# Routing moved into the output stage of a decoder block, tile by tile, with its slot table summed on TensorE

## What is computed

```
xn = rms_norm(h);  proj = xn @ w_in                       # 1024 -> 4352
m  = sigmoid(g_a) * (swa(q_a,k_a,v_a) @ P_a) + sigmoid(g_b) * (stick_breaking(q_b,k_b,v_b) @ P_b)
h  = h + m @ w_out
h  = h + moe_ffn(rms_norm(h))

moe_ffn: logits = x @ router_w + router_b                 # 32 experts
         top_logit, top_idx = top_k(logits, 4);  gate = softmax(top_logit)
         per expert e and its tokens:
             gu = x @ w_gate_up[e] + b_gate_up[e]         # 1024 -> 2048
             act = (clip(u, -7, 7) + 1) * (min(g, 7) * sigmoid(1.702 * min(g, 7)))
             out[token] += gate * (act @ w_down[e] + b_down[e])
```

## Time and profile before

| | |
|---|---|
| median of 3 runs | 2639.85 us |
| the profiled execution | 2638.29 us, its span 2636.7 us |
| mean granted TensorE clock | 0.946 |
| TensorE busy | 2372.2 us (90%) |
| VectorE busy | 1606.5 us (61%) |
| ScalarE busy | 1310.4 us (50%) |
| GpSimd busy | 907.4 us (34%) |
| HBM read and written | 480.34 MB, 47.56 MB |

### The profile page before, as it was taken

The page is one execution under the profiler, slowest core; times in us unless marked ns, Lnnn a source line. Parts: engine busy times, 40 slices in busy tenths (PEclk is TensorE's granted clock), DMA queues, the critical chain, the costliest instruction groups (busy, mean ns, idle before and its releaser), DMA issues.

```text
span 2636.7 us, 39181 instructions
## 1 busy us (share of the span) xinstructions
PE 2372.2 (90%) x13878; PEld 1822.8 (69%) x13879; DVE 1606.5 (61%) x1526; ACT 1310.4 (50%) x1453; POOL 907.4 (34%) x654
## 2 busy tenths in 40 slices
PE   6989999999998889029999999999999999999995
PEld 5857768777786768017777777777777777777774
DVE  4034353544423432727878887878888878777785
ACT  4145454554534421025655665556566556555554
POOL 1210101011011100762545454545465535434453
PEclk9988989999898989559999999999999999999998
DMA  3000201111114432348888998889899888887884
GB/s 128 25 25 21 65 22 41 47 30 58 36 57 156 138 136 104 94 150 307 323 290 304 344 326 290 303 297 367 280 367 347 280 290 319 291 281 273 298 303 149
DMA packets 277825, 524.72 MB, mean 199 GB/s; under 512 B 39041, under 2 KB 87228, under 8 KB 277596
## 3 DMA queue, kind: packets, MB, share of 16 engines
q1 hardware_dynamic: 244028, 476.21, 50.9%
q0 software_dynamic: 22208, 43.38, 6.9%
q10 hardware_dynamic: 11520, 4.20, 0.6%
HBM read 480.34 MB, written 47.56 MB: 200 GB/s over the span
## 4 chain that ended last, share of the span: by engine, by line
PE 41%; POOL 6%; issue 5%; DMA 3%; ACT 1%; DVE 1%; POOLq 0%; DVEq 0%; ACTq 0%
PE ex_gu L1790 23%; PE ex_yp L1834 8%; PE ex_rest L1812 4%; DMA ex_nxt<-slots 3%; PE ex_rest L1851 2%; POOL ex_idx L1576 2%; PE ex_gu L1783 1%; POOL slots L1563 1%; ACT ex_whi L1491 1%; POOL ex_nxt L1571 1%; POOL ex_sel L1618 1%; PE ex_tr L1751 1%; DVE ex_hlo L1681 1%; PE ex_yp L1827 0%; ACT ex_hhi L1510 0%
## 5 line engine op out<-in xcount | busy, mean ns | idle before, releaser
L1648 DVE TENSOR_TENSOR ex_wlo<-ex_raw,ex_whi 128x2048 fp32r<-128x2048 f32 x355 | 804.6, 2291 | 179.1 <-ACT ex_whi L1491 177.9
L1491 ACT ACTIVATE ex_whi<-ex_raw 128x2048 fp32r<-128x2048 f32 x387 | 736.0, 1920 | 311.9 <-PE ex_gu L1790 224.4
L1790 PE MATMUL ex_gu<-ex_whi,ex_xhi 128*128 128x512 f32 x1024 | 333.9, 407 | 5.4 <-DVE ex_wlo L1648 5.4
L1790 PE MATMUL ex_gu<-ex_wlo,ex_xhi 128*128 128x512 f32 x1024 | 321.0, 395 | 0.0
L1790 PE MATMUL ex_gu<-ex_whi,ex_xlo 128*128 128x512 f32 x1024 | 319.6, 393 | 0.0
L603 POOL TENSOR_TENSOR at_wlo<-at_raw,at_whi 128x1024 fp32r<-128x1024 f32 x32 | 79.6, 2487 | 583.8 <-ACT at_whi L448 583.8
L1629 POOL TENSOR_TENSOR ex_wlo<-ex_raw,ex_whi 128x2048 fp32r<-128x2048 f32 x32 | 148.0, 4625 | 251.9 <-ACT ex_whi L1491 251.9
L1790 PEld LDWEIGHTS ex_gu<-ex_whi,ex_xhi 128*128 128x128 f32 x1024 | 192.2, 189 | 58.0 <-DVE ex_wlo L1648 7.4
L1790 PEld LDWEIGHTS ex_gu<-ex_whi,ex_xlo 128*128 128x128 f32 x1024 | 193.9, 189 | 43.9
L1790 PEld LDWEIGHTS ex_gu<-ex_wlo,ex_xhi 128*128 128x128 f32 x1024 | 193.6, 189 | 42.9
L56 PE MATMUL at_job<-xnT_hi,at_whi 128*128 128x512 f32 x448 | 196.1, 438 | 0.0
(11 more groups left out here) (256 smaller groups left out, 4198.7 us busy)
## 6 DMA issues: line engine op xcount, KB each, us to landing
ex_raw<-in_w_gate_up_dram SPq DMA_DIRECT2D x512, 512.0 KB, 7.0
ex_raw<-in_w_down_dram SPq DMA_DIRECT2D x256, 512.0 KB
at_raw<-in_w_in_dram SPq DMA_DIRECT2D x28, 512.0 KB
gT<-at_gst SPq DMA_DIRECT2D x32, 256.0 KB, 2.4
mg_g<-gT SPq DMA_DIRECT2D x32, 256.0 KB, 3.1
n_x<-in_x_dram SPq DMA_DIRECT2D x8, 512.0 KB, 8.1
mg_ytok<-y_s SPq DMA_DIRECT2D x16, 256.0 KB, 4.2
raw_o<-in_w_out_dram SPq DMA_DIRECT2D x8, 512.0 KB, 6.6
```

The lines of the kernel that those rows point to most:

```text
L1491: nc.scalar.activation(w_hi[:, i % RING, :], raw[:, i % SLABS, :], ACT.Copy).then_inc(hi_d, 1)
L1648: nc.vector.tensor_tensor(w_lo[:, slot, :], raw[:, i % SLABS, :], w_hi[:, slot, :].bitcast(F32), ALU.subtract).then_inc(lo_d, 1)
L1790: mm = nc.tensor.matmul(gu[:, half, h, :], x[:, k, :], w[:, kk, h, :], start=k == 0 and n == 0, stop=k == KD - 1 and n == 2)
```

## The change

Routing is no longer a stage. Its parts go to four places. In `project_values` GpSimd makes the bias pieces, which are stored to HBM and loaded again in the expert stage. In the output stage each tile is routed as soon as its logits are there: `choose` (top 4, one-hot rows), `rank_tokens` (ranks on TensorE), `hand_out` (weights, and the one-hot matrix of slots) and `take_slots`, four float32 products that add (token, weight) at (expert, slot) into a table in PSUM. The slots of an expert up to its 160th are then on the chip, and `next_rows` copies them instead of loading them. The table of further blocks (`further_table`, `destinations`) is computed by VectorE in expert blocks 0 and 1, and the 32 scatters to HBM are issued four at a time in blocks 2 to 9; they are read only in block 30. The merge has seven buffers for eight, `us` and `us2` are gone (their contents stand in `hid`, `hid2`).

```diff
 (project_values, sync and gpsimd)
             def _(sp):
                 load_first_tiles(sp, w_in, raw, raw_in)
+                for q in range(3):
+                    sp.dma_start(brow[q * NE:(q + 1) * NE, 0:2 * D], b_gate_up[0, :, :]).then_inc(b_in, 16)
+                    sp.dma_start(brow[q * NE:(q + 1) * NE, 2 * D:3 * D], b_down[0, :, :]).then_inc(b_in, 16)
+                sp.wait_ge(b_d, 13)
+                sp.dma_start(bp_s[:, :], pieces[:, :]).then_inc(b_in, 16)
+                sp.wait_ge(b_in, 112)
+            @block.gpsimd
+                step(nc.gpsimd.memset(bp[3 * NE:P, :], 0.0))
+                step(nc.gpsimd.memset(pick[:, :], 0.0))
...
 (merge)
-                    after(sp, tr_mm, n - 7)
-                    sp.dma_start(ytok[:, n % 8, :], y_s[a, t * P:(t + 1) * P, :]).then_inc(y_in[n % 8], 16)
+                    after(sp, tr_mm, n - 6)
+                    sp.dma_start(ytok[:, n % 7, :], y_s[a, t * P:(t + 1) * P, :]).then_inc(y_in[n % 7], 16)
...
 (output stage, vector)
+                def choose(t):
+                    dve.wait_ge(lg_ev, t + 1)
+                    step(nc.vector.max(top[:, t, :], logits[:, t, :]))
+                    step(nc.vector.max_index(idx[:, t, :], top[:, t, :], logits[:, t, :]))
+                    nc.vector.tensor_tensor(ex[:, t, :], top[:, t, 0:TOPK], top[:, t, 0:1].to_broadcast([P, TOPK]),
+                                            ALU.subtract).then_inc(ex_d, 1)
+                    step(nc.vector.tensor_copy(which[:, t, :], idx[:, t, 0:TOPK]))
+                    step(nc.vector.tensor_tensor(oh[:, t % 2, :, :], same(iota_e[:, :], NE), each(which[:, t, :], NE),
+                                                 ALU.is_equal))
+                    step(nc.vector.tensor_reduce(chosen[:, :], oh[:, t % 2, :, :].rearrange("p j e -> p e j"), AX_X, ALU.add))
+                    nc.vector.tensor_copy(chosen16[:, t, :], chosen[:, :]).then_inc(ch_d, 1)
+                def hand_out(t):
+                    s = t % 2
+                    dve.wait_ge(rk_mm, t + 1)
+                    nc.vector.tensor_tensor(prod[:, :, :], oh[:, s, :, :], same(lg[:, 2 * NE:3 * NE], NE), ALU.mult)\
+                        .then_inc(rk_ev, 1)
+                    dve.wait_ge(rk_ev, t + 1)
+                    step(nc.vector.tensor_reduce(rank[:, t, :], prod[:, :, :], AX_X, ALU.add))
+                    after(dve, sl_mm, t - 1)
+                    step(nc.vector.tensor_tensor(is_slot[:, s, :, :], same(iota_s[:, :], 2 * P), each(rank[:, t, :], 2 * P),
+                                                 ALU.is_equal))
+                    step(nc.vector.tensor_scalar(held[:, s, :, 0, :], oh[:, s, :, :], tokf[:, t:t + 1], None, ALU.mult))
+                    dve.wait_ge(a_exp, t + 1)
+                    ...
+                    nc.vector.tensor_tensor(held[:, s, :, 1, :], oh[:, s, :, :], each(mine, NE), ALU.mult).then_inc(sl_d, 1)
                 for t in range(NT):
                     if t + 1 < NT:
                         residual(t + 1)
+                    if t:
+                        hand_out(t - 1)
+                    if t + 1 < NT:
                         normalize(t + 1)
                     dve.wait_ge(lg_mm, t + 1)
                     nc.vector.tensor_tensor(logits[:, t, :], lg[:, 0:NE], rbB[:, :], ALU.add).then_inc(lg_ev, 1)
+                    choose(t)
+                hand_out(NT - 1)
+                step(nc.vector.tensor_copy(rt["counts"][:, :], lg[:, 3 * NE:4 * NE]))
+                step(nc.vector.tensor_copy(rt["loads"][:, :], rt["counts"][0:1, :]))
+                dve.wait_ge(sl_mm, NT)
+                step(nc.vector.tensor_copy(rt["table"][:, :], table[0:2 * NE, 0:2 * P]))
 (output stage, tensor)
+                def rank_tokens(t):
+                    pe.wait_ge(ch_d, t + 1)
+                    for b in range(t + 1):
+                        last = nc.tensor.matmul(lg[:, 2 * NE:3 * NE], (upper if b == t else ones)[:, :], chosen16[:, b, :],
+                                                start=b == 0, stop=b == t)
+                    ...
+                def take_slots(t):
+                    pe.wait_ge(sl_d, t + 1)
+                    for j in range(TOPK):
+                        last = nc.tensor.matmul(table[0:2 * NE, 0:2 * P],
+                                                held[:, t % 2, j, :, :].rearrange("p c e -> p (c e)"),
+                                                is_slot[:, t % 2, j, :], start=t == 0 and j == 0,
+                                                stop=t == NT - 1 and j == TOPK - 1)
+                    last.then_inc(sl_mm, 1)
                     last.then_inc(lg_mm, 1)
+                    if t:
+                        take_slots(t - 1)
                     if t + 2 < NT:
                         project(t + 2, 1)
+                    rank_tokens(t)
+                take_slots(NT - 1)
...
 (experts, gpsimd)
-            def next_rows(b):
+            def next_rows(b, on_chip=True):
...
-                load_slots(b)
-                hold(pool, idx_in, 16 * (1 + Q) * (b + 1), spare)
+                if on_chip:
+                    nc.gpsimd.tensor_copy(nxt[:, :, :].rearrange("p h c -> p (h c)"),
+                                          tab[:, bass.ds(b, 1), :].rearrange("p o c -> p (o c)")).then_inc(nxt_d, 1)
+                    hold(pool, nxt_d, b + 1, spare)
+                else:
+                    load_slots(b)
+                    hold(pool, idx_in, 16 * (1 + Q) * (b - NE + 1), spare)
...
                                         ALU.mult, ALU.add).then_inc(piece_d, 1)
+                if t is not None:
+                    if t == 0:
+                        hold(pool, dest_d, 1, spare)
+                    scatter(t)
                 hold(pool, hi_d, SLABS * b + POOLED + 1, spare)
...
+            for b in range(2 + NT):
+                body(b, False, first=b == 0, t=b - 2 if b >= 2 else None)
 (experts, vector)
             body(0, False, first=True)
-            nov = over_blocks(dve, body, first=1)
+            further_table()
+            body(1, False)
+            destinations()
+            nov = over_blocks(dve, body, first=2)
```

More of the change, by code:

```diff
@@ L90, in norm_and_transpose @@
         tr = ctx.enter_context(nc.psum_tensor("n1_tr", [P, 4, HALF], F32))
-        x_in = [sem(f"n1_x_in{t}") for t in range(NT)]
         w_in_ = sem("n1_w_in")
@@ L874, in merge @@
         tr = ctx.enter_context(nc.psum_tensor("mg_tr", [P, 4, HALF], F32))
-        y_in = [sem(f"mg_y_in{s}") for s in range(8)]
         raw_in = [sem(f"mg_raw_in{s}") for s in range(2)]
@@ new lines, in _ @@
+                for d in range(Q):
+                    nc.gpsimd.memset(quarter[d * CAP2:(d + 1) * CAP2, 0:1], float(d)).then_inc(c_set, 1)
+                pool.wait_ge(c_set, 4 + Q)
+                nc.gpsimd.iota(blank[:, :, 0], [[1, CAP]], base=T, channel_multiplier=0).then_inc(c_set, 1)
+                nc.gpsimd.affine_select(out=upper[:, :], in_=upper[:, :], compare_op=ALU.is_gt, fill=0.0, base=0,
+                                        pattern=[[1, P]], channel_multiplier=-1).then_inc(c_set, 1)
@@ L1091, in _ @@
+                pool.wait_ge(c_set, 14 + Q)
+                nc.gpsimd.tensor_scalar(place[:, 1:2], place[:, 1:2], float(P), None, ALU.add).then_inc(c_set, 1)
+                pool.wait_ge(c_set, 15 + Q)
+                for h in range(2):
+                    nc.gpsimd.tensor_scalar(spare_row[:, h, :], place[:, h:h + 1].to_broadcast([P, NE]), float(T), None,
+                                            ALU.add).then_inc(c_set, 1)
+                    pool.wait_ge(c_set, 16 + Q + h)
                 for t in range(NT):
@@ L1143, in project @@
                         last.then_inc(mm_done, 1)
+                def rank_tokens(t):
[3 more added lines that the diff above has]
+                                                start=b == 0, stop=b == t)
+                    if t == NT - 1:
+                        for b in range(NT):
+                            last = nc.tensor.matmul(lg[:, 3 * NE:4 * NE], ones[:, :], chosen16[:, b, :], start=b == 0,
+                                                    stop=b == NT - 1)
+                    last.then_inc(rk_mm, 1)
+                def take_slots(t):
[6 more added lines that the diff above has]
+                    last.then_inc(sl_mm, 1)
+                pe.wait_ge(c_set, 10)
                 for t in range(2):
@@ L1609, in next_rows, with body @@
                 gather()
+            pool.wait_ge(tab_d, 2)
             next_rows(0)
             next_rows(1)
-            def body(b, over, first=False):
+            def body(b, over, first=False, t=None):
                 e = over_expert(pool, b) if over else b
@@ L1630, in body @@
                                         ALU.subtract).then_inc(lo_pool, 1)
-                next_rows(b + 2)
-            body(0, False, first=True)
-            nov = over_blocks(pool, body, first=1)
+                if isinstance(b, int) and b == NE - 2:
```

(25 more changed lines are left out.)

408 lines of the change are left out of this document (204 added, 204 removed).

## The result

The changed kernel takes 2547.9 us (median of 4 runs, 2546.2 to 2548.5) against 2641.1 us in the runs beside it: ratio 0.965, 95% interval 0.963 to 0.968. That is 3.5% faster. The profiled execution has a span of 2546.9 us against 2636.7, 89.8 less; the sum had said 66.8.

What follows compares the result with a forecast made beforehand. TensorE, busy 90% of the span, was taken as the bound, with one 92.3 us wait for the first expert gather. Terms -76.0 + 16.5 - 7.3 = -66.8 us gave 2572 us; 8-in-10 range 2551 to 2601.

Steps and rivals of the forecast that it cites:

- The hole: TensorE's stretch from R to the first expert product, with its gather wait: from 123.3 to 47.3 us, shrinking by 76.0.
- R: Moment in the output stage when the last output projection is done and tile 6's transposes start.
- rival 3: Better than thought: 2.4 GHz in the tail (-5), gather in 8.4 (-3), scatters hidden (-10): 2554 us; chance 0.12.
- Paid before R: Work added ahead of R in the value, output and merge code, (a) to (d) together: +16.5 us.
- (a): Output stage: slot products added on TensorE per tile, 2.3 us for each of five tiles before R: +11.5 us.
- (b): Value projection: GpSimd's bias work there meets the eight splits that TensorE waits for: +2.5 us, between 0 and 6.
- (c): Merge: seven instead of eight token buffers make a load wait for one more transpose group: +1.5 us, between 0 and 3.
- (d): Output stage: constants, a 1280-column memset and others, made beside the first splits: +1 us, between 0 and 3.
- Expert stage: Expert blocks: selector waits removed (-14.6 and -2.7), scatters added in blocks 2 to 9 (+10): net -7.3 us.
- Rival 1: First expert gather lands behind the weights, 20 instead of 11.5 us, and the tail is slow: 2585 us; chance 0.20.
- Rival 2: Scatters in blocks 2 to 9 take 3.8 us each, costing 39 instead of 10: 2601 us; chance 0.14.
- rival 4: GpSimd bounds blocks 2 to 9; from 5.0 us per scatter the remaining gain is gone; chance 0.03, with anything slower.

Runs made afterwards that it cites:

- experiment 5: Changed kernel with all weight loads of block 0 held back until the first expert gather has landed; 2547.1 us.
- experiment 1: Changed kernel, but for experts 12 to 31 GpSimd again loads the slot columns from the table in HBM; 2564.7 us.
- experiment 4: Kernel before, with only the bias pieces made by GpSimd in the value projection, stored, and loaded at the routing stage's start; 2610.6 us.
- experiment 2: Changed kernel with GpSimd writing a block's selector after the first, or after both, accumulating scatters instead of ahead of them; 2601.6 and 2716.4 us.
- 2538.6: Changed kernel with a block's four scatters moved from ahead of GpSimd's split to behind the next gather; 2538.6 us.
- 2529.3: Changed kernel with VectorE's split of the second hidden half ahead of its split of slab 11; 2529.3 us.
- 2545.5: Changed kernel with late scatters, earlier hidden split, last tile's ranks first, and the constants' wait moved to the first rank product; 2545.5 us.

## Why the prediction missed, step by step

**The hole, forecast 47.3 us, measured 43.2.** Right within 4. The gather landed 11.5 us after the expert stage began, exactly the value taken, and experiment 5 shows why it is not 8.4: the weights. Transposes to first product took 7.1 against 7.8. What was off is the walk of the tail, 24.5 us instead of 28 (the table out at R+24.0 instead of R+27.7). I priced all of it at the 1.2 GHz level, but for tile 7 the eight transposes took 1.07 us and the 16 router products 2.91, not 1.97 and 3.62; from R to the table the granted clock was 0.73 on the mean. It was the clause of rival 3, and with the splits some 4 us of the miss.

**Paid before R, forecast +16.5, measured +9.4.** (a) was right: +10.6 from the residual of tile 1 to R against 11.5; eight passes take 1.94 us, as the earlier trace rows said, and the period became 15.7 against 15.9. (b), (c) and (d), together +5, came to -1.1. For (b) the splits took 6.01 us against 5.97 with GpSimd's memset (2.65 us) and selects beside them, so the term is zero: the lower bound, not the 2.5 taken. For (d) TensorE now waits 7.3 us for the constants at the output stage's start instead of 6.05 for a split, and its later waits there are shorter. The residual of tile 1 began between 961.2 and 967.9, and the first gather's transposes between 1087.4 and 1096.7, in eight traces of code that is the same up to there, so these small terms can't be told apart, and part of these 7 us may be such spread.

**Expert stage, forecast -7.3, measured -19.1.** This is where the prediction failed most, by 11.8 us of 23, in one term: "of 17.3 us of waits 2.7 (block 0) and up to 14.6 go". It gave each wait its own length, and put the rest of a block, in which nothing was changed, at nothing. Both steps failed. Without scatters the stage is 28.7 us shorter than before (1440.0 to 1411.3), 11.4 more than the waits. Those 11.4, from the periods:

- 6.6 us lie evenly over the blocks: the 17 that had no wait for the selector are 0.21 us shorter on the mean (49.0 to 48.8, 40.9 to 40.7), and I count as much in each of 31.
- 3.4 us are the lower clock, in blocks 14 and 17 alone: waits of 2.57 and 2.58 us were worth 4.4 and 4.5, of which 0.2 each is counted above. Experiment 1 brings this back.
- 1.2 us are in block 0, within its spread.
- 1.5 us are in the other blocks with waits (0.38, 2.58 and eight of 0.80 us), a little over the length of each.
- Block 2 takes 1.4 back: it became 1.1 us longer.

The first of these is in the products themselves, at a granted clock of 1.00 in both. The first and the last of twelve pairs of products in block 26, before:

```profile
2336.41 0.62 PE L1790 MATMUL ex_gu<-ex_whi,ex_xhi 128*128 128x512 f32 x2
...
2341.44 0.63 PE L1790 MATMUL ex_gu<-ex_whi,ex_xlo 128*128 128x512 f32 x2
```

and after:

```profile
2249.28 0.61 PE L1895 MATMUL ex_gu<-ex_whi,ex_xhi 128*128 128x512 f32 x2
...
2254.27 0.61 PE L1895 MATMUL ex_gu<-ex_whi,ex_xlo 128*128 128x512 f32 x2
```

From start to start that is 5.03 us before and 4.99 after. It is 5.03 in experiment 4, whose expert stage is the old one, and 4.99 in experiment 1, where selector waits are back, so it does not come from the waits. No run shows what it does come from.

The lower clock behind a wait, which experiments 1 and 2 show, is thus less than a third of what this term missed. The scatters were right as a sum, 9.4 us against 10, by luck: they took 1.3 us each (with the gap 1.45 to 1.7) instead of 2.3, but blocks 4, 6 and 8 lost 4.8 instead of 3.9, blocks 2 and 3 lost 3.2 instead of 6.3, and 1.4 lie in blocks 0 and 10, which have no scatters. The slack of 7.9 us did not hold, because a VectorE operation is held by the pushed split before the slab is wanted.

**The rivals.** Rival 1 (gather behind the weights) was seen in kind, 7.0 instead of 3.7 us, and its loss is already in the 11.5. Rival 2 and rival 4 rested on 3.8 and 5.0 us a scatter; none took over 2.94 in after. Rival 3 (2554) had the right sign in its first clause, but the scatters were not hidden. What no rival named is that a wait can be worth more than its length, and that the products themselves could become faster.

**The two rules.** The trace of after shows VectorE's 128x512 product at 3.22 us beside GpSimd's subtraction, and the value stage's splits untouched beside a memset. The Trainium skill ("SBUF — State Buffer", section SBUF: two separate sides) has the finer rule that the prediction should have used in place of the general one: the shared port is locked for a whole instruction by whichever starts first, and a VectorE operation with two SBUF inputs competes only with a GpSimd operation that reads SBUF. By it (b)'s memset costs nothing, and the trace agrees. For the scatters the row shows 0.98 us alone and 2.92 beside a two-input subtraction. The Trainium skill ("DMA: Bandwidth & Descriptors", section SWDGE vs HWDGE vs iDMA) names only the two-port mode as what locks descriptor writing out; here an issue was held beside a plain two-input operation. Whether it was the writing of descriptors or the reading of the indices that waited, no run shows.

## What to carry to other kernels

Price a removed wait of TensorE by the block's period with and without it, not by its length: here 2.6 us of wait was worth up to 4.5 where the clock fell behind it and, block 0 aside, 3.2 at most where it did not, and 31.5 us of waits for the hidden split were worth 18.6. Compare a block without any wait in both traces first, to see what the rest of the change did to every block. Before moving work to GpSimd look for the stretch in which it waits for a DMA, not only for slack before its next deadline: the same 32 scatters cost 9.4 us in front of its split, nothing behind the gather as long as the selector is not late, and nothing behind the accumulating scatters even in the shortened blocks. Two moves that use the same slack do not add (2538.6 and 2529.3 gave 2545.5 together).

## What was not expected of the hardware

Waits of 2.6 to 2.7 us were followed by 1.00 of the clock or by 4.7 us at 0.64, both in one and the same trace, that of before. The same products ran 0.8% faster in the expert stage of the changed kernel (4.99 us against 5.03) at the same granted clock. A scatter's issue on GpSimd that begins while VectorE's two-input 128x2048 split runs ends 0.8 us after that split (2.92 us against 0.98). Holding 4 MB of weights back behind a gather of 0.6 MB halved the gather's landing (3.7 us against 7.0) and did not move the first product beyond the spread of equal code.
